# A two-layer decoder trunk on one core: the router computed by token tile in plain float32, split gates for the expert slots, one output unit in place of two, the queries' input in buffers of its own, and softmax norms head by head

## The reference, cut to what matters

```
h = hybrid_mixer(x, ...)            # projections, four head groups, then y @ w_out
x = layer_norm(ALPHA * x + h, ...)
q = x @ wq;  k = mem @ wk;  v = mem @ wv          # 4 heads of 256, 256 memory tokens
p = softmax(q k^T / 16);  h = (p v) @ wo
x = layer_norm(ALPHA * x + h, ...)
scores = sigmoid(x @ router_w);  sel = scores + router_b
# best group of 4 experts by the sum of its top 2 sel, then the top 2 experts in it
gates = scores of those two, divided by their sum
h = sum over e of gates[:, e] * ((silu(x @ w_gate[e]) * (x @ w_up[e])) @ w_down[e])
x = layer_norm(ALPHA * x + h, ...)
```

## Time and profile before

| | us |
|---|---|
| median of three runs | 798.44 (797.78 to 798.54) |
| profiled execution, its own time | 797.88 |
| span of its instructions | 796.1 |
| TensorE busy (matmul row) | 737.6 |
| VectorE busy | 404.1 |
| ScalarE busy | 279.3 |

### The profile page before, as it was taken

One profiled execution on the slowest core, in us unless ns is written; L12 is line 12 of the kernel. 1 busy time (PEld: TensorE's weight loads), 2 busy tenths in 40 slices (PEclk: granted clock), 3 DMA queues, 4 the chain that ended last, 5 costly groups with the idle time before them and its releaser, 6 DMA issues.

```text
span 796.1 us, 12438 instructions
## 1 busy us (share of the span) xinstructions
PE 737.6 (93%) x5004; PEld 597.4 (75%) x5004; DVE 404.1 (51%) x703; ACT 279.3 (35%) x480; POOL 46.2 (6%) x88
## 2 busy tenths in 40 slices
PE   4999999999898989999799989999998989899992
PEld 3979888779787966555499789878897888655651
DVE  4685894763537512112468587757444573121115
ACT  4455642543524111111244565334543231211111
POOL 3400000000004100000020000001000000000000
PEclk9999999999999999999999999999999999999997
DMA  9991235664229259999975331457540652799971
GB/s 277 349 307 55 80 89 203 212 211 160 105 95 388 51 212 354 419 414 415 364 270 161 109 107 54 131 196 238 176 173 39 238 238 88 305 388 418 417 287 56
DMA packets 62529, 176.13 MB, mean 221 GB/s; under 512 B 3856, under 2 KB 37056, under 8 KB 53248
## 3 DMA queue, kind: packets, MB, share of 16 engines
q1 hardware_dynamic: 57856, 162.80, 55.5%
q0 software_dynamic: 4032, 12.24, 4.6%
q10 hardware_dynamic: 576, 0.20, 0.1%
HBM read 174.18 MB, written 1.05 MB: 220 GB/s over the span
## 4 chain that ended last, share of the span: by engine, by line
PE 79%; DVE 10%; issue 3%; ACT 3%; DVEq 2%; DMA 1%; POOL 0%; ACTq 0%; POOLq 0%; SPq 0%
PE ring L1821 14%; PE ring L1854 7%; PE ring L1458 7%; PE ring L1460 7%; PE ring L1459 7%; PE quad L1458 6%; PE quad L1460 5%; PE quad L1459 5%; PE quad L1866 4%; PE ring L1728 2%; PE ring L1707 2%; DVE w_lo L894 2%; PE quad L1771 2%; PE quad L1772 1%; PE ring L1606 1%
## 5 line engine op out<-in xcount | busy, mean ns | idle before, releaser
L894 DVE TENSOR_TENSOR w_lo<-raw,w_hi 128x1024 fp32r<-128x1024 f32 (+1 forms) x116 | 133.0, 1186 | 82.5 <-ACT w_hi L618 78.7
L1458 PE MATMUL ring<-x_hi,w_hi 128*128 128x256 f32 x480 | 141.3, 294 | 11.1 <-issue 4.3
L618 ACT CAST w_hi<-raw 128x1024 fp32r<-128x1024 f32 (+1 forms) x116 | 112.6, 1020 | 82.1 <-PE quad L1460 73.6
L1459 PE MATMUL ring<-x_lo,w_hi 128*128 128x256 f32 x480 | 137.8, 287 | 0.0
L1460 PE MATMUL ring<-x_hi,w_lo 128*128 128x256 f32 x480 | 137.8, 287 | 0.0
L1458 PEld LDWEIGHTS ring<-x_hi,w_hi 128*128 128x128 f32 x480 | 94.1, 196 | 14.4 <-issue 6.6
L1459 PEld LDWEIGHTS ring<-x_lo,w_hi 128*128 128x128 f32 x480 | 94.2, 196 | 0.6 <-issue 0.5
L1460 PEld LDWEIGHTS ring<-x_hi,w_lo 128*128 128x128 f32 x480 | 93.9, 196 | 0.0
L641 ACT ACTIVATE arena<-ring 128x512 f32<-128x512 f32 (+1 forms) x68 | 36.5, 567 | 90.9 <-PE ring L1460 74.0
L1385 DVE TENSOR_TENSOR y_lo<-ring,y_hi 128x512 fp32r<-128x512 f32 x32 | 22.1, 692 | 72.9 <-ACT y_hi L849 72.9
L1458 PE MATMUL quad<-w_hi,y_hi 128*128 128x512 f32 x144 | 57.1, 397 | 0.0
(11 more groups left out here) (294 smaller groups left out, 1303.7 us busy)
## 6 DMA issues: line engine op xcount, KB each, us to landing
raw<-in_moe_w_gate SPq DMA_DIRECT2D x20, 1024.0 KB, 6.4
raw<-in_moe_w_up SPq DMA_DIRECT2D x16, 1024.0 KB, 8.6
w_raw<-in_moe_w_up SPq DMA_DIRECT2D x16, 1024.0 KB, 10.8
w_raw<-in_moe_w_down SPq DMA_DIRECT2D x16, 1024.0 KB, 10.6
raw<-in_w_in SPq DMA_DIRECT2D x14, 1024.0 KB, 11.3
raw<-in_moe_w_down SPq DMA_DIRECT2D x12, 1024.0 KB, 9.6
raw<-in_xattn_wk SPq DMA_DIRECT2D x8, 1024.0 KB, 6.0
raw<-in_w_out SPq DMA_DIRECT2D x8, 1024.0 KB, 4.9
```

Of the source, the lines that this page charges most:

```text
L618: nc.scalar.copy(unit_slot(u, 0, n)[:, s], raw[:, SLOT[u], s]).then_inc(hi_done, 1)
L894: low = nc.vector.tensor_tensor(unit_slot(u, 1, n)[:, s], raw[:, SLOT[u], s], unit_slot(u, 0, n)[:, s].bitcast(F32), ALU.subtract)
L1458: mm(out, a_hi, b_hi, start=first, stop=False)
L1459: mm(out, a_hi, b_lo, start=False, stop=False)
```

## The change

Six things are changed.

1. The last two output units of one chunk each become one of two chunks, so a layer has one unit less and all later ones move by one in both rotations (six raw slots, two split slots).
2. In the first LayerNorm, `stats(0)` stands after the split of the first value unit, and the splits of k3, of the value units and the affines alternate in another way.
3. x for the queries is turned between the third and fourth value unit and split into `xb_hi`, `xb_lo`, which lie in free parts of `arena`. Two splits move from ahead of that to behind it.
4. In cross-attention, DVE takes max of head h + 1, then the norm of head h. The split of the second output unit (`ahead(U_Q + 3)`) moves behind all norms.
5. The router works by token tile: the turned x is moved whole (float32, `xT`), eight float32 products per tile put the tokens on rows with 16 columns (`logits`), and ACT takes exp of them. `rw` is kept in float32, without parts. `xn_lo` of the second tile is taken in two halves behind the first one-hot, and the first gather has another order (`gather_first`) so that its last products come late.
6. `half_gates` are half the gates as high and low float32r parts (two more DVE operations), `gates_of_slots` multiplies these with 4 columns in float32r, and DVE adds the parts.

```diff
-OUT_CHUNKS = [(6, 2), (0, 2), (8, 2), (2, 2), (4, 1), (5, 1)]
+OUT_CHUNKS = [(6, 2), (0, 2), (8, 2), (2, 2), (4, 2)]
...
-    jobs += [(f"xc{i}", "dve") for i in range(4)]
-    jobs += [("rt0", "act"), ("rt1", "act")]
+    jobs += [("xc0", "act"), ("xc1", "act"), ("rt0", "act"), ("xc2", "act"), ("xc3", "dve"), ("rt1", "act")]
...
+        xT = x_slots[:, 0, :, :]
-        rw = sb("rw", [P, 3 * P], F32R)
+        rw = sb("rw", [P, DC, E])
+        half_gates = sb("half_gates", [P, T, PAIRS, 4], F32R)
+        xb_hi = rounded("xb_hi", 9216, DC, SEQ)
+        xb_lo = rounded("xb_lo", 0, DC, SEQ)
...
-                    sp.wait_ge(unit_used, used(U_MOE - SPLIT_SLOTS + (SLOT[u] - RAW_SLOTS) // 2, l))
+                    last = max(v for v in range(U_MOE) if v % SPLIT_SLOTS == (SLOT[u] - RAW_SLOTS) // 2)
+                    sp.wait_ge(unit_used, used(last, l))
...
-                for i in range(3):
+                for i in range(2):
                     ahead(U_V + i)
-                x_high("xb", l)
-                ahead(U_V + 3)
+                x_high("xb", l, xb_hi)
+                for i in range(2, 4):
+                    ahead(U_V + i)
...
-                x_high("xc", l)
-                for t in range(T):
+                def turned_x(j):
+                    t, c = j // 2, 4 * (j % 2)
+                    move(f"xc{j}", l, xT[:, c:c + 4, t * P:(t + 1) * P], bank(f"xc{j}").rearrange("p (a b) -> p a b", a=4))
+
+                def logits_exp(t):
+                    act.wait_ge(misc_ready, misc_done(f"rt{t}", l))
+                    nc.scalar.activation(rt[:, 1, t, :], bank(f"rt{t}")[:, 0:E], ACT.Exp, scale=-1.0).then_inc(act_emptied, 1)
+
+                def rows_high(t):
                     nc.scalar.copy(xn_hi[:, t], X[:, t, :].rearrange("p (q c) -> p c q", c=DC)).then_inc(xn_hi_done, 1)
-                move("rt0", l, logitsT, bank("rt0")[:, 0:SEQ])
-                act.wait_ge(misc_ready, misc_done("rt1", l))
-                nc.scalar.activation(rt[:, 1], bank("rt1")[:, 0:SEQ].rearrange("p (t e) -> p t e", t=T)[:, :, 0:E],
-                                     ACT.Exp, scale=-1.0).then_inc(act_emptied, 1)
-
+
+                turned_x(0)
+                turned_x(1)
+                rows_high(0)
+                logits_exp(0)
+                turned_x(2)
+                rows_high(1)
+                logits_exp(1)
...
                 add(0)
-                stats(0)
+                if meanwhile is None:
+                    stats(0)
                 dve.wait_ge(done, count)
                 add(1)
-                if meanwhile[0]:
+                if meanwhile:
                     meanwhile[0]()
+                    stats(0)
+                    meanwhile[1]()
...
                 layer_norm(0, l, unit_used, used(U_K_LATE - 1, l),
-                           (lambda: (ahead(U_K_LATE - 1), ahead(U_K_LATE)), lambda: ahead(U_V)))
-                for u in range(U_V + 1, U_V + 3):
-                    ahead(u)
-                x_low("xb", l, 2)
-                ahead(U_V + 3)
-                for i in range(4):
+                           (lambda: ahead(U_K_LATE - 1), lambda: ahead(U_K_LATE), lambda: ahead(U_V)))
+                ahead(U_V + 1)
+                x_low("xb", l, 2, None, xb_hi, xb_lo)
+                for i in range(2, 4):
+                    ahead(U_V + i)
+                for i in range(3):
                     ahead(U_Q + i)
...
                 layer_norm(1, l, unit_used, used(U_O + 3, l))
-                x_low("xc", l, 3)
-                for t in range(T):
+                dve.wait_ge(misc_ready, misc_done("xc3", l))
+                nc.vector.tensor_copy(xT[:, 4:8, P:2 * P], bank("xc3").rearrange("p (a b) -> p a b", a=4)).then_inc(dve_emptied, 1)
+
+                def rows_low(t, chunks):
                     dve.wait_ge(xn_hi_done, l * T + t + 1)
-                    last = nc.vector.tensor_tensor(xn_lo[:, t], X[:, t, :].rearrange("p (q c) -> p c q", c=DC),
-                                                   xn_hi[:, t].bitcast(F32), ALU.subtract)
-                last.then_inc(xn_lo_done, 1)
+                    nc.vector.tensor_tensor(xn_lo[:, t, chunks, :],
+                                            X[:, t, :].rearrange("p (q c) -> p c q", c=DC)[:, chunks, :],
+                                            xn_hi[:, t, chunks, :].bitcast(F32), ALU.subtract).then_inc(xn_lo_done, 1)
+
+                rows_low(0, slice(0, DC))
...
                 nc.vector.tensor_tensor(gates[:], weight, view(grp[:, 0, 10:12], [[1, T], [0, E]]), ALU.mult)
+                dve.drain()
+                of_pairs = gates[:].rearrange("p t (j e) -> p (t j) e", e=2)
+                halves = half_gates[:].rearrange("p t j e -> p (t j) e")
+                nc.vector.tensor_scalar(halves[:, :, 0:2], of_pairs, 0.5, None, ALU.mult)
+                dve.drain()
+                nc.vector.scalar_tensor_tensor(halves[:, :, 2:4], of_pairs, 0.5, halves[:, :, 0:2].bitcast(F32), ALU.mult,
+                                               ALU.subtract)
                 dve.drain().then_inc(gates_ready, 1)
...
                 one_hot(0)
+                rows_low(1, slice(0, DC // 2))
+                rows_low(1, slice(DC // 2, DC))
...
-                out_unit(4, 6)
-                out_unit(5, 7)
+                out_unit(4, 7)
                 project("xk3", K_UNITS[3], l)
 
                 pe.wait_ge(quad_free, l * (3 * T) + T)
                 for i in range(4):
+                    if i == 3:
+                        transpose_x("xb", l, 1)
                     into_quad(x_hi, x_lo, 2 * i, 2, U_V + i, l, i == 0, i == 3, values=True)
-                transpose_x("xb", l, 1)
                 pe.wait_ge(dve_emptied, emptied("xb3", l))
                 for i in range(4):
-                    project(f"xq{i}", U_Q + i, l)
+                    project(f"xq{i}", U_Q + i, l, xb_hi, xb_lo)
...
+                def logits(t):
+
+                    o = free(f"rt{t}", l)
+                    for k in range(DC):
+                        r = mm(o[:, 0:E], xT[:, k, t * P:(t + 1) * P], rw[:, k, :], start=k == 0, stop=k == DC - 1)
+                    r.then_inc(misc_ready, 1)
...
+                    pe.wait_ge(xn_lo_done, l * 3 + 1)
+                    pe.wait_ge(slots_ready, l * 4 + 1)
+                    for k in range(0, DC, 2):
+                        but_last(k)
+                    for h in range(2):
+                        pe.wait_ge(xn_lo_done, l * 3 + 2 + h)
+                        for k in (4 * h, 4 * h + 2):
+                            part(k, 1, xn_lo, last=True)
+                        for k in (4 * h + 1, 4 * h + 3):
+                            but_last(k)
+                            part(k, 1, xn_lo, last=True).then_inc(gathered, 1)
...
-                                r = mm(ring[:, 3, 2 * j:2 * j + 2], to_slot(t)[:, j * P:(j + 1) * P].bitcast(F32),
-                                       gates[:, t, 2 * j:2 * j + 2], start=t == 0, stop=t == T - 1)
+                                r = mm(ring[:, 3, 4 * j:4 * j + 4], to_slot(t)[:, j * P:(j + 1) * P],
+                                       half_gates[:, t, j, :], start=t == 0, stop=t == T - 1)
```

102 lines of the change are left out of this document (54 added, 48 removed).

## The result

The changed kernel takes 775.14 us (median of four executions, 773.49 to 776.84), against 798.49 (797.78 to 803.03) for the kernel before, measured beside it. The ratio is 0.9696, with a 95% interval of 0.9655 to 0.9738. The forecast was 776.4, with a range of 771.5 to 783.5. The profiled executions took 797.88 and 775.23, so 22.65 us went; the sum of the prediction was 22.0. The total fits, but cross-attention gave 2.6 us less than forecast, and 1.5 came from a stage that the sum had at nothing, and that part is luck.

The account below looks back on a forecast made before the run. TensorE, busy 93% of the span, bounds the kernel: only its idle time, lower clock or removable work can be won. Terms 3.7 + 3.7 + 1.5 + 3.5 + 6.2 + 3.4 = 22.0 us; forecast 776.4 against 798.4, range 771.5 to 783.5.

Parts of the forecast that it names:

- One output unit and the LayerNorm's order: TensorE's waits ahead of k3 (0.87 us) and the first value unit (0.97) go: 1.84 a layer, 3.7 in both.
- Turning x between the value units: TensorE's wait for x_lo ahead of the queries goes: 3.7 us in both layers, plus 1.5 of clock in layer 1.
- Softmax by heads: In cross-attention, less waiting and a holding clock gain 1.75 us a layer, 3.5 in both; bounds 0.55 and 2.1.
- The wait: In cross-attention, only 0.55 us of TensorE's 1.80 is won, because ScalarE's first move is late next.
- The clock: In cross-attention, the clock holds for the first probabilities-by-values product; the fall costs 1.5 us, of which 1.2 was counted.
- rival (a): Clock still falls in cross-attention and once more at a new place: 2.4 + 1.5 us back, 780.3; chance 0.17.
- The router: From the second tile's turning, counts start at 9.9 us; the gather starts 3.2 and 3.0 us earlier, 6.2 together.
- Rival (c): Router gives half: logits, ScalarE's order or gather's covers each slip about 1 us a layer, 782.4; chance 0.14.
- The gates: Gates of the slots take 16 float32r records in about 1.8 us, not 32 in 3.47: gain 3.4 in both layers.
- Rival (b): Transposes inside the values' product do not count as busy, so the clock falls: 2 x 1.5 back, 779.4; chance 0.05.
- (d): LayerNorm edits only move the waits in front of the fourth value unit: 3.7 and 1.5 back, 781.6; chance 0.04.
- (e): Slower than before: behind the new places the clock stays at 1.2 GHz; 20 such stretches give 806; chance 0.02.

Follow-up runs that it names:

- plain gates: Changed kernel with the gates of the slots by 32 plain float32 records again, without half_gates: 787.77 us, ratio 0.984.
- wide products between them: The plain gates kernel with a 128-column identity product behind every second pair of gate products, four more in all: 785.42 us, ratio 0.9796.
- late turning: Changed kernel with x turned behind the fourth value unit again and the value units' splits in their old order: 782.98 us, ratio 0.9774.
- early statistics: Changed kernel with the first tile's statistics ahead of the second add again, one large last output unit kept: 774.54 us, ratio 0.967.
- two units: Changed kernel with two small last output units again, the new order around the LayerNorm kept: 775.5 us, ratio 0.9684.
- both edits out: Changed kernel with two small last output units and the statistics ahead of the second add, both together: 779.25 us, ratio 0.9724.
- early xn_lo: Changed kernel with both halves of the second tile's xn_lo ahead of the sigmoid, not behind the first one-hot: 780.47 us, ratio 0.9774.
- the four without it: Changed kernel with 14 identity products in the gap (773.9 us); first head turned and moved early (770.96); plus turned_move(0) early (765.52); plus seven identity products (764.83).

## Why the prediction was right, and where it was not

**One output unit and the LayerNorm's order: right in size, wrong in who does it.** 1.84 a layer was forecast; 2.26 came, of which 0.32 is what the idle figures of rows 3 leave out, 0.16 for each of the two waits; the last 0.1 is not traced. The step "now ... the second add ends near 144.0, the low part follows at once" held to 0.1 us (low part at 144.00), but the move of the statistics was counted as needed. Without it nothing comes back; without the large unit alone, one wait does; without both, two do.

**Turning x between the value units: right.** 2.02 and 2.03 instead of 1.85, for the same 0.16, and 1.59 of clock in layer 1 for 1.5. Undone, it costs the gap and the fall.

**Softmax by heads: the term that was mis-sized.** 1.75 a layer was forecast, 0.45 and 0.49 came. Three steps stood in it, and the third failed. The wait: 0.55 was forecast and about 0.45 came, with ScalarE late next as described, its move at 203.86. The gap's length: the prediction has "one of about 1.5"; it is one of 1.91. The clock: "I take it that the clock then holds" failed in both layers:

```profile
204.60 3.31 PE L1760 MATMUL ring<-arena 128*128 128x256 f32 x8 [1.91 <-ACT arena L641]
```

```profile
205.06:208.47 3.41, 3.41 (x11) 2.71 (x11) 2.10 (x2) 0.52 (x1) 0.00 (x0) 0.50 0.30 38
583.94:587.35 3.41, 3.41 (x12) 2.75 (x11) 2.58 (x4) 0.98 (x2) 0.00 (x0) 0.50 0.19 24
```

The gaps before, 1.80 and 0.33 us in layer 1, had become one of 1.91: the total idle time shrank, the longest gap did not. This is the first half of rival (a). Its second half, a fall at a new place, did not come true in the span that counts; instead the one in the experts' stage of layer 1 is gone. The idle time ahead of the third product is the same 2.20 us in both kernels; first TensorE's row of the kernel before, then that of the changed one:

```profile
293.28 5.32 PE L1821 MATMUL ring<-raw,x_slots 128*64 128x256 f32 x32 [2.20 <-ACT arena L842]
```

```profile
281.88 3.67 PE L1882 MATMUL ring<-raw,x_slots 128*64 128x256 f32 x32 [2.20 <-ACT arena L851]
```

That is 1.65 us, of which 0.14 are lost again up to the first output unit of layer 2. Nothing in the change bears on that wait, and behind it the clock fell in 10 of 24 layers (the kernel before, the changed kernel and the ten experiments that keep it). So the 1.5 is luck: without it 21.2 would have come. The range had room for a fall or two less; the sum did not. A fall of 6.83 us at 13.91 is new, but costs nothing: the first output unit starts at 112.23 as at 112.26 before.

**The router: right, to 0.3.** 3.2 and 3.0 were forecast, 3.24 and 3.30 came. From the second turning the counts were to start 9.9 us later; it is 254.19 - 244.57 = 9.62. The timeline of TensorE behind the second tile's logits: the filler, the counts and the gather, which waits 0.16 for VectorE.

```profile
244.57 1.12 PE L1549 MATMUL ring<-ident,X 128*128 128x128 f32 x8
...
246.52 1.93 PE L1770 MATMUL ring<-rw,x_slots 128*128 128x16 f32 x16 [0.16 <-issue]
248.30 6.05 PE L1532 MATMUL ring<-ident 128*128 128x128 f32 x52
254.19 0.31 PE L1791 MATMUL ring<-arena,before 128*128 128x32 f32 x2
...
256.97 0.36 PE L1818 MATMUL ring<-y_hi,xn_hi 128*128 128x256 f32 x1 [0.16 <-DVEq L1371]
```

VectorE starts the sigmoid 4.1 us behind that turning (4.4 forecast), and sixteen records with 16 columns start 1.78 us ahead of what follows (1.84 forecast). Rival (c) had each cover slip by a microsecond; none did. No run takes the router's new form out as a whole: its gain is read from the two timelines, and only the place of VectorE's xn_lo was tried by itself.

**The gates: right in the count, not in the worth.** 1.79 and 1.70 of 1.7. The first and last of sixteen records, and the first expert product behind them:

```profile
264.56 0.17 PE L1857 MATMUL ring<-half_gates,y_hi 128*128 128x4 f32 x1
...
266.15 0.25 PE L1857 MATMUL ring<-half_gates,y_lo 128*128 128x4 f32 x1
...
266.33 0.87 PE L1882 MATMUL ring<-raw,x_slots 128*64 128x256 f32 x6
```

Taken out of the changed kernel the item costs 12.6 us, not 3.5, by the clock. Rival (b) found nothing to stand on. Rivals (d) and (e) did not occur: no wait stands ahead of the fourth value unit, and the mean clock is 0.979.

In the profiled executions 22.0 were forecast and 22.7 came: -2.6 in cross-attention, +1.5 in the experts' stage, +0.8 at the output unit, +0.3 each at the turning of x and in the router, +0.2 of clock, +0.1 for the gates. What stays open is why the clock falls behind one gap of 1.91 us and not behind the next, and why the plain float32 gates let the clock fall in both layers of two kernels and in neither layer of the kernel before.

## What to carry to other kernels

Measure a step from start to start of the same products in both timelines, and price a gap by its length and, apart from that, by the fall of the clock that may follow it. Do not take a smaller sum of idle time for a clock that holds: here the sum shrank, the longest gap grew by 0.1 us, and the falls stayed. What decides over a fall is not shown, so give it a chance and not a yes or no. Where two edits are aimed at the same wait, ask whether either alone removes it. If a gap can't be removed, look for the engine that is late next before reordering, here ScalarE's move behind the last exponential: that move was worth 3.24 us a layer with the clock, and the reordering 0.45 to 0.49.

## What was not expected of the hardware

- **The fall behind a gap comes and goes.** In eight profiles with the gap of 1.91 us (the changed kernel, and those with plain gates, wide products between them, late turning, early statistics, two units, both edits out, early xn_lo) the clock fell behind it in 11 of 16 layers; in the four without it, in none of 8. A fall costs 1.68 us there (9.35 against 7.67). The length of the gap alone does not decide: behind the wait of 2.20 us in the experts' stage it fell in 10 of 24 layers, and behind the idle 1.69 us at the turning of the memory in layer 2 in 12 of 13 profiles, in layer 1 in 2 of the same 13.
- **It can come with no gap at all.** In the plain gates the clock fell to 0.50 with TensorE busy in every one of the 3.45 us before (by the modelled ends; the starts stand 0.22 apart per two records), and stayed there for 6.85.
- **It can hide work in a total.** Two output units cost 1.24 us a layer in waits, and the median rose by 0.4; the falls in cross-attention were missing in that profile.
- **Executions differ by it, and not by it alone.** The changed kernel's took 773.49 us at a mean clock of 0.984 and 775.05 to 776.84 at 0.979.
- **A full identity product in float32 costs 0.23 us** as two records (28 in 3.29 us), and one with 16 columns hardly less: the eight of a tile start 1.78 us ahead of what follows.
